# A narrower router and a gather spread over PSUM banks in a two-layer transformer kernel with experts

## The reference, cut to what matters

```python
logits = (xt @ w_router).astype(jnp.float32)          # 256 x 8
top_vals, top_idx = lax.top_k(logits, TOP_K)          # TOP_K = 2
top_w = jax.nn.softmax(top_vals, axis=-1)
combine = jnp.sum(jax.nn.one_hot(top_idx, N_EXPERTS, dtype=jnp.float32) * top_w[..., None], axis=1)
y = jnp.zeros_like(xt)
for e in range(N_EXPERTS):                            # 8 experts, hidden size 3584
    y = y + combine[:, e:e + 1] * swiglu(xt, w_gate[e], w_up[e], w_down[e])
```

## Time and profile before

| what | us |
|---|---|
| median of 3 runs | 2569.75 (2567.75 to 2573.59) |
| profiled execution | 2568.69, of which the span 2566.9 |
| busy in it: TensorE matmuls | 2358.2 (92%) |
| busy in it: DVE / ACT / POOL | 1809.4 / 1436.2 / 76.7 |
| expert layer, from the first router matmul to the end of the span | 1515.7 to 2566.9 |
| first matmul of the first expert | 1549.0 |

### The profile page before, as it was taken

How to read it: one execution, slowest core, us unless ns; L and a number is a source line. 1 busy time by engine, 2 the same in 40 slices (tenths; PEclk the granted TensorE clock), 3 DMA queues, 4 the chain that set the end, 5 groups by cost and what they waited for, 6 DMA issues and landing times. The chain is left out here.

```text
span 2566.9 us, 30070 instructions
## 1 busy us (share of the span) xinstructions
PE 2358.2 (92%) x11132; PEld 1970.0 (77%) x11132; DVE 1809.4 (70%) x2497; ACT 1436.2 (56%) x2065; POOL 76.7 (3%) x71
## 2 busy tenths in 40 slices
PE   6788999967899899899989879999999999999997
PEld 5677787757788778678877777888888888888885
DVE  4955555784555556655555647989898989898987
ACT  4433444442444444444444436878787878787875
POOL 0200000110000100000010000000000000000000
PEclk9867999985899999999999969999999999999998
DMA  6402555420455553445553326999999999999996
GB/s 238 135 1 83 195 188 182 148 90 1 150 188 188 186 169 103 140 166 191 185 186 122 123 82 240 368 340 369 340 377 338 371 347 368 341 371 341 365 347 234
DMA packets 157176, 570.81 MB, mean 222 GB/s; under 512 B 18497, under 2 KB 18817, under 8 KB 156385
## 3 DMA queue, kind: packets, MB, share of 16 engines
q1 hardware_dynamic: 153424, 553.48, 61.1%
q0 software_dynamic: 3600, 15.35, 1.8%
HBM read 567.71 MB, written 1.05 MB: 222 GB/s over the span
## 5 line engine op out<-in xcount | busy, mean ns | idle before, releaser
L369 DVE TENSOR_TENSOR w_lo<-raw,w_hi 128x1024 fp32r<-128x1024 f32 x1051 | 1270.0, 1224 | 444.0 <-ACT w_hi L363 416.6
L363 ACT CAST w_hi<-raw 128x1024 fp32r<-128x1024 f32 x1051 | 1098.9, 1052 | 474.4 <-PE bank L417 453.7
L415 PE MATMUL bank<-w_hi,x_hi 128*128 128x512 f32 (+1 forms) x2864 | 1136.4, 397 | 44.0 <-DVE x_lo L455 23.7
L417 PE MATMUL bank<-w_hi,x_lo 128*128 128x512 f32 (+1 forms) x2864 | 1116.1, 390 | 0.0
L416 PE MATMUL bank<-w_lo,x_hi 128*128 128x512 f32 (+1 forms) x2864 | 1114.2, 389 | 0.0
L415 PEld LDWEIGHTS bank<-w_hi,x_hi 128*128 128x128 f32 x2864 | 544.8, 190 | 154.1 <-issue 25.0
L417 PEld LDWEIGHTS bank<-w_hi,x_lo 128*128 128x128 f32 x2864 | 543.3, 190 | 113.0
L416 PEld LDWEIGHTS bank<-w_lo,x_hi 128*128 128x128 f32 x2864 | 545.6, 191 | 104.1
L748 PE MATMUL bank<-arena,PT 128*128 128x64 f32 (+1 forms) x576 | 96.2, 326 | 2.2 <-DVE O L765 2.2
L706 ACT ACTIVATE PP<-bank,small 128x256 f32<-128x256 f32 x80 | 37.2, 470 | 107.8 <-DVE small L696 107.8
L748 PEld LDWEIGHTS bank<-arena,PT 128*128 128x128 f32 x576 | 93.6, 247 | 2.6 <-DVE PT L735 2.4
(11 more groups left out here) (185 smaller groups left out, 1391.6 us busy)
## 6 DMA issues: line engine op xcount, KB each, us to landing
raw<-in_stream SPq DMA_DIRECT2D x1051, 512.0 KB, 5.7
tab<-in_lngb POOLq DMA_DIRECT2D x5, 1024.0 KB, 5.2
arena<-in_rpb POOLq DMA_DIRECT2D x16, 256.0 KB, 5.1
arena<-in_bgate POOLq DMA_DIRECT2D x4, 512.0 KB, 4.6
tab<-in_rowv POOLq DMA_DIRECT2D x2, 640.0 KB, 9.2
X<-in_x SPq DMA_DIRECT2D x1, 1024.0 KB, 5.4
out_y<-X SPq DMA_DIRECT2D x2, 512.0 KB, 2.9
tab<-in_ropec POOLq DMA_DIRECT2D x2, 448.0 KB, 5.1
```

The lines of the kernel that those rows point to most:

```text
L363: nc.scalar.copy(w_hi[:, s % SPLIT, :], raw[:, slot, :]).then_inc(hi_done, 1)
L369: e.tensor_tensor(w_lo[:, s % SPLIT, :], raw[:, s % RAW, :], w_hi[:, s % SPLIT, :].bitcast(F32), ALU.subtract).then_inc(lo_done, 1)
L415: pe.matmul(out, xh, wh, start=first, stop=False)
L417: return pe.matmul(out, xl, wh, start=False, stop=last)
```

## The change

Three edits go together.

- The router weights lie in one tile `rw` of 128 x 8 x 16: for each feature block 8 high columns and 8 low ones beside them. One matmul of 16 columns takes the place of two of 8, 32 matmuls instead of 64. The sums of high and low columns are then 16 numbers for each token block, both blocks in bank 0, and one `tensor_reduce` on DVE adds each pair in place of the two copies.
- The six gather pieces of the first expert rotate over banks 0, 4, 5, 2, 4, 5 (right halves). TensorE waits for `xe_lo` no longer ahead of pieces 1 to 3, and ahead of pieces 4 and 5 only for the piece that used their bank before.
- The first matmul of the first expert waits for four pieces (the `x_lo` blocks) instead of six.

The wait for `ye_ready` in `if part` belongs to the second pass, which does not run.

```diff
-        rw_hi = sb("rw_hi", [P, KD, NE], F32R)
-        rw_lo = sb("rw_lo", [P, KD, NE], F32R)
+        rw = sb("rw", [P, KD, 2 * NE], F32R)
...
             if E.kind == "act":
-                nc.scalar.copy(rw_hi[:, :, :], router[:, :, :]).then_inc(
-                    rw_split, 1)
+                nc.scalar.copy(rw[:, :, 0:NE], router[:, :, :]).then_inc(rw_split, 1)
             if E.kind == "dve":
                 e.wait_ge(rw_split, 1)
-                e.tensor_tensor(rw_lo[:, :, :], router[:, :, :],
-                                rw_hi[:, :, :].bitcast(F32), ALU.subtract).then_inc(rw_split, 1)
+                e.tensor_tensor(rw[:, :, NE:2 * NE], router[:, :, :], rw[:, :, 0:NE].bitcast(F32),
+                                ALU.subtract).then_inc(rw_split, 1)
...
                 for tb in range(TB):
                     t = slice(tb * P, (tb + 1) * P)
-                    n = 0
+                    o = bank[0][:, tb * 2 * NE:(tb + 1) * 2 * NE]
                     for k in range(KD):
-                        for a in (x_hi, x_lo):
-                            for b in (rw_hi, rw_lo):
-                                i = e.matmul(bank[tb][:, 0:NE], a[:, k, t], b[:, k, :], start=n == 0,
-                                             stop=n == 4 * KD - 1)
-                                n += 1
+                        e.matmul(o, x_hi[:, k, t], rw[:, k, :], start=k == 0, stop=False)
+                        i = e.matmul(o, x_lo[:, k, t], rw[:, k, :], start=False, stop=k == KD - 1)
                 i.then_inc(lg_full, 1)
             if E.kind == "dve":
                 e.wait_ge(lg_full, 1)
-                for tb in range(TB):
-                    i = e.tensor_copy(lg[:, tb * 8:(tb + 1) * 8], bank[tb][:, 0:NE])
-                E.link(i)
+                E.link(e.tensor_reduce(lg.rearrange("p (t n) -> p t n", t=TB), bank[0][:, 0:4 * NE].rearrange(
+                    "p (t a n) -> p t n a", t=TB, a=2), AX.X, ALU.add))
...
-        def gather_piece(E, p, buf):
+        def gather_piece(E, p, buf, out=bank[2][:, 2 * P:4 * P]):
             e = E.e
-            out = bank[2][:, 2 * P:4 * P]
...
+            banks = (0, 4, 5, 2, 4, 5)
             for p in range(pieces):
                 n = part * pieces + p + 1
+                out = bank[banks[p]][:, 2 * P:4 * P]
                 if E.kind == "pe":
                     if p == 0:
                         e.wait_ge(se_ready, part * (NE + 1) + 1)
-                    else:
-                        e.wait_ge(xe_lo, n - 1)
-                    gather_piece(E, p, 0).then_inc(xe_full, 1)
+                        if part:
+                            e.wait_ge(ye_ready, NE)
+                    elif p >= KD // 2:
+                        e.wait_ge(xe_lo, n - 3)
+                    gather_piece(E, p, 0, out).then_inc(xe_full, 1)
...
             if E.kind == "pe":
-                e.wait_ge(xe_lo, (part + 1) * pieces)
+                e.wait_ge(xe_lo, part * pieces + KD // 2)
```

More of the change, by code:

```diff
@@ L1553, in experts @@
                         e.wait_ge(se_ready, part * (NE + 1) + 1)
-                    else:
-                        e.wait_ge(xe_lo, n - 1)
-                    gather_piece(E, p, 0).then_inc(xe_full, 1)
+                        if part:
[3 more added lines that the diff above has]
+                    gather_piece(E, p, 0, out).then_inc(xe_full, 1)
                 if E.kind == "act":
                     e.wait_ge(xe_full, n)
-                    gather_piece(E, p, 0).then_inc(xe_hi, 1)
+                    gather_piece(E, p, 0, out).then_inc(xe_hi, 1)
                 if E.kind == "dve":
                     e.wait_ge(xe_hi, n)
-                    i = gather_piece(E, p, 0)
+                    i = gather_piece(E, p, 0, out)
                     (i if i is not None else e.engine_nop()).then_inc(xe_lo, 1)
             if E.kind == "pe":
-                e.wait_ge(xe_lo, (part + 1) * pieces)
+                e.wait_ge(xe_lo, part * pieces + KD // 2)
             s0 = E.st.s
```

## The result

The changed kernel takes 2551.55 us (median of 4 runs, 2549.98 to 2552.17), against 2568.75 us for the kernel before beside it (2566.85 to 2573.59). The ratio is 0.9929 with a 95% interval of 0.9912 to 0.9946, so the kernel is faster by 17.2 us, and by 14 to 23 us within the interval. The forecast was 13.9 us less and 2555.8 us. The measured time lies just inside the low end of the stated range, 2551.5 to 2562.0.

The account below looks back on a forecast made before the run. TensorE's matmuls bound the expert stage, so the gain lies in starting it earlier: 6.83 + 0.05 + 5.4 + 1.65 = 13.9 us, profiled execution 2554.8 us, median 2555.8 us, range 2551.5 to 2562.0.

Parts of the forecast that it names:

- Router, 6.83 + 0.05: Router: 32 removed matmuls at a pitch of 0.214 us give 6.83 us; one reduce replacing two copies gives 0.05.
- Gather, 5.4: First expert's gather: pieces 0 to 3 run without waits, so the expert starts 5.4 us sooner.
- pieces 4 and 5 fit behind piece 3's round: Gather's end: the last two pieces' loads, 1542.40 to 1543.06, fit inside piece 3's round, which ends at 1543.59.
- Clock in the first chunk, 1.65: First expert's chunk 0: no clock fall at the gather's end, so its 24 matmuls run at full clock, gaining 1.65 us.
- The wait for it stays, and with it I expect the fall near 1559.8: First expert: TensorE's 1.99 us wait for the first silu remains, and the clock falls there again; no gain counted.
- a rival at 0.16: First expert: the clock fall behind the first silu goes too, another 1.65 us, 2554.2 us; chance 0.16.
- The end is the same work: Kernel's end: last scatter, layer norm and output are the same work; no gain counted.
- the half clock through gather and chunk 0: Gather and first expert's chunk 0: clock stays at half, total gain only 7.8 us, 2562.0 us; chance 0.10.
- the dear 16 columns: Router: matmuls of 16 columns cost twice those of 8, so it gains nothing, 2562.7 us; chance 0.05.
- the unchanged round: Gather: ACT or DVE sets the round, pieces still follow at 2.08 us, 2559.4 us; chance 0.05.
- the stream as the bound: Expert stage: weight loads at 363 GB/s become the limit, costing 28 us against 13.9 gained, 2584 us; chance 0.02.

Follow-up runs that it names:

- e7_busy: Changed kernel plus useless 512-column matmuls on TensorE, 34 ahead of the transposes and 12 behind the router; 2550.56 us.
- e3_wait_six: Changed kernel, but the first expert waits for all six gather pieces again instead of four; 2551.96 us.
- e2_gather_only: Changed kernel with the router put back to 64 matmuls of 8 columns and its copies, keeping the new gather; 2558.42 us.
- e1_router_only: Changed kernel with the gather put back in bank 2 with all its waits, keeping the new router; 2560.63 us.
- e6_shift4: Changed kernel plus 4 unused 16-column matmuls behind the router, 0.85 us later; 2555.08 us.
- e5_shift8: Changed kernel plus 8 unused 16-column matmuls behind the router, 1.71 us later; 2553.98 us.
- e5_shift16: Changed kernel plus 16 unused 16-column matmuls behind the router, 3.41 us later; 2553.84 us.
- e10_all: Changed kernel with router operands exchanged, silu table loaded early, and 34 useless matmuls ahead of the transposes; 2547.14 us.
- e9_swap: Changed kernel with the router's operands exchanged: 16 router columns loaded, 256 tokens moved, 16 matmuls of 256 columns; 2549.49 us.

## Why the prediction was right where it was, and wrong where it was not

- *Router, 6.83 + 0.05:* right. 6.87 us measured, the pitch 0.214 with 16 columns as with 8, the reduce 0.19 us (0.19 forecast). The Trainium skill, page "TensorE: Matmul & The Clock Gate", section "LDWEIGHTS (loading the stationary operand)", has 107 ns for a load of 128 columns. The pitch in e7_busy at full clock is 0.11 us, which agrees; at half clock it is 0.214, which the section's one figure does not give.
- *Gather, 5.4:* right, 5.41, and pieces 4 and 5 fit behind piece 3's round as worked out (e3_wait_six: 0.05 us).
- *Clock in the first chunk, 1.65:* right, 1.62. The fall at the gather's end went with the gather's waits (e2_gather_only), and the router alone leaves it there (e1_router_only). At the matmul behind the silu the forecast of 13.9 met 13.90.
- *"The wait for it stays, and with it I expect the fall near 1559.8":* this step failed. The wait stayed, 1.99 us, and the fall did not come: 1.26 + 0.46 = 1.72 us that I had given as a rival at 0.16. That rival's reason, a shorter wait and denser matmuls, is not what the runs show either. I took the wait as the cause of the fall. The shifts show that its moment decides as well, so that the changed kernel missed the fall was luck: the same wait brings a fall in e6_shift4 and none in the changed kernel, e5_shift8 and e5_shift16.
- *"The end is the same work":* true of the work, wrong of the time. The last scatter took 4.40 us before and 2.48 after, another 1.92. Over all 14 profiles it took from 2.34 to 5.31, with the same eight matmuls behind the same wait of 2.80 us. Where it took under 2.6 us the clock fell over 5 us behind its first matmul, elsewhere from 0.7 us ahead of it to 1.8 us behind. A fall at its first matmul costs about 1.2 us (3.71 in e1_router_only against 2.48); the other 0.7 us of the kernel before are its pause of 0.4 us, and a clock that stays at half to the end, while in e1_router_only it is back at 1.00 before the final layer norm starts. That the changed kernel had neither is luck as far as the runs show. With the second fall this is the whole difference between 13.9 and 17.5, and the measured time stayed inside the range because the range had room for one of the two and for scatter.
- *Rivals:* the half clock through gather and chunk 0 did not come; nor did the dear 16 columns, the unchanged round, or the stream as the bound: e1_router_only has 987.25 us from the first transposes to the last scatter against 987.15 before, so the stream gives back or takes nothing. The half-clock rival has chunk 0 longer by 1.8 us without a working; by the prediction's own pitch of 0.43 us, 23 distances make 9.9 us, 2.9 more than the 6.96 before.
- *The range* had 2.5 us on the low side for the scatter of medians. It should have held both lucky cases of the clock at once, 13.9 + 1.7 + 1.9 us.

What stays open: why the clock's moments keep the same distance to the router from one execution to the next although the stretch ahead varies by 9 us. Each kernel has one trace, so that the pattern repeats within a kernel is not shown; kernels that are alike up to the moment agree. And no run takes apart the pauses within the last scatter, 0.4 us in the kernel before (0.21 us idle put down to "issue") and 1.36 us in e2_gather_only.

## What to carry to other kernels

When a result goes from TensorE over ACT and DVE and back, count the rounds and not the busy times: four pieces in four banks cost about one round and three times TensorE's own part (0.89 us), where in one bank they cost about four rounds of 2.08. In a row of small matmuls (fp32r, up to 256 columns at half clock here) count matmuls, not columns; and if one operand is narrow, load that one and move the wide one. A gap on TensorE has two prices, its length and a fall of the clock that it may bring: give the second one a range of its own for each gap, at the kernel's end too, and compare kernels by distances within a trace when code ahead of the change scatters by more than the change brings.

## What the runs showed of the hardware that I had not expected

- A matmul's pitch at half clock is 0.214 us from 8 to 256 moving columns (fp32r, 128 columns loaded), and 0.43 at 512.
- Behind a wait of 1.69 us the granted clock fell 0.8 us into matmuls of 16 columns and stayed at half through the 5 us of them that followed (e7_busy). Behind the same wait it stayed at 1.00 through 1.9 us of matmuls of 256 columns (e10_all). From half clock it rose behind 3.1 us of matmuls of 256 columns (e9_swap), and did not rise within 6.6 us of 16 columns in the changed kernel.
- The same idle stretch of 1.99 us brought a fall of the clock or none by its moment: 4 more matmuls ahead brought it, 8 or 16 did not. A shift of 0.85 us cost 2.19 us.
- With the same eight matmuls behind the same wait of 2.80 us, the last scatter took 2.34 to 5.31 us, by where the clock's fall lay and by a pause of up to 1.36 us.
